# Both attention layers' work items issued in another order, fillers of TensorE included

## The reference, cut to what matters

```python
for layer in range(DEPTH):                      # DEPTH = 2
    h = h + hybrid_mixer(rms_norm(h, attn_norm[layer]), positions, layer, w_in[layer], ...)
    hn = rms_norm(h, ffn_norm[layer])
    h = h + (swiglu(hn, ...) if layer % 2 == 0 else moe_ffn(hn, ...))
return rms_norm(h, final_norm)

def hybrid_mixer(h, ...):
    (q_a, k_a, v_a, q_i, k_i, w_i, q_b, k_b, v_b, c_q, c_kv, k_r) = split(h @ w_in)
    o_a = dsa_attention(q_a, k_a, v_a, q_i, k_i, w_i)   # top 64 keys of a score, by w_i
    o_b = diff_attention(q_b, k_b, v_b, lam, ...)       # softmax minus lam * softmax, then a norm
    o_c = mla_attention(q_nope, q_rope, k_nope, k_rope, v_c)
    return concat(o_a, o_b, o_c) @ w_out
```

## Time and profile before

| | |
|---|---|
| median of 3 runs | 1509.1 us (1507.15 to 1510.11) |
| the profiled execution | 1507.44 us |
| its span, first to last instruction | 1505.7 us |
| PE busy | 1479.6 us (98%) |
| DVE busy | 1233.9 us (82%) |
| ACT busy | 1036.7 us (69%) |
| attention of layer 0 | from the start to about 149 us |
| dense part | to about 388 us |
| attention of layer 1 | to about 538 us |
| experts | from there to the end |

### The profile page before, as it was taken

One profiled execution on the slowest core, in us unless ns is written; L12 is line 12 of the kernel. 1 busy time (PEld: TensorE's weight loads), 2 busy tenths in 40 slices (PEclk: granted clock), 3 DMA queues, 4 the chain that ended last, 5 costly groups with the idle time before them and its releaser, 6 DMA issues.

```text
span 1505.7 us, 18848 instructions
## 1 busy us (share of the span) xinstructions
PE 1479.6 (98%) x7112; PEld 1233.6 (82%) x7112; DVE 1233.9 (82%) x1499; ACT 1036.7 (69%) x1355; POOL 107.9 (7%) x185
## 2 busy tenths in 40 slices
...
GB/s 286 204 57 57 244 178 213 168 196 151 126 169 92 58 239 395 374 358 400 358 370 391 366 364 396 356 362 376 382 368 388 371 372 371 384 382 369 414 389 114
DMA packets 46317, 436.86 MB, mean 290 GB/s; under 512 B 4112, under 2 KB 10640, under 8 KB 22032
## 3 DMA queue, kind: packets, MB, share of 16 engines
...
...
## 4 chain that ended last, share of the span: by engine, by line
PE 95%; DVE 3%; ACT 1%; issue 1%; DMA 0%; POOL 0%; POOLq 0%; ACTq 0%; SPq 0%; DVEq 0%
PE pair L936 51%; PE work L936 34%; PE work L908 3%; PE pair L1006 2%; PE pair L908 2%; PE work L1080 1%; PE work L923 1%; PE work L1214 1%; DVE arena L1727 0%; ACT w_hi L1306 0%; DMA ring<-in_w_in 0%; DVE w_lo L1659 0%; DVE nmax L1758 0%; DVE arena L1744 0%; ACT arena L1324 0%
## 5 line engine op out<-in xcount | busy, mean ns | idle before, releaser
L1659 DVE TENSOR_TENSOR w_lo<-ring,w_hi 128x1024 fp32r<-128x1024 f32 (+3 forms) x810 | 960.9, 1215 | 199.3 <-ACT w_hi L1306 186.1
L1306 ACT ACTIVATE w_hi<-ring 128x1024 fp32r<-128x1024 f32 (+3 forms) x810 | 838.5, 1052 | 300.8 <-PE pair L936 123.8
L936 PE MATMUL pair<-w_hi,hnT_hi 128*128 128x512 f32 x672 | 265.1, 395 | 1.7 <-DVE hnT_lo L2026 0.9
L936 PE MATMUL pair<-w_hi,hnT_lo 128*128 128x512 f32 x672 | 262.0, 390 | 0.0
L936 PE MATMUL pair<-w_lo,hnT_hi 128*128 128x512 f32 x672 | 261.5, 389 | 0.0
L936 PE MATMUL work<-w_hi,hidT_hi 128*128 128x512 f32 x552 | 215.1, 390 | 2.6 <-DVE hidT_lo L1960 1.4
L936 PE MATMUL work<-w_lo,hidT_hi 128*128 128x512 f32 x552 | 214.8, 389 | 0.0
L936 PE MATMUL work<-w_hi,hidT_lo 128*128 128x512 f32 x552 | 214.8, 389 | 0.0
L936 PE MATMUL pair<-w_hi,xU_hi 128*128 128x512 f32 x448 | 177.1, 395 | 0.0
L936 PE MATMUL pair<-w_hi,xU_lo 128*128 128x512 f32 x448 | 174.8, 390 | 0.0
L936 PE MATMUL pair<-w_lo,xU_hi 128*128 128x512 f32 x448 | 174.3, 389 | 0.0
...
## 6 DMA issues: line engine op xcount, KB each, us to landing
...
```

Source lines behind the costliest of these rows:

```text
L936: mm = pe.matmul(b, lhs[x_part][k + kk], w[w_part][:, kk, :], start=(first and kk == 0 and i == 0), stop=(last and kk == 1 and i == 2))
L1306: return act.activation(o, i, ACT.Copy)
L1659: dve.tensor_tensor(lo, raw, hi.bitcast(F32), ALU.subtract).then_inc(lo_done, 1)
```

## The change

The strings in `LISTS` are replaced by others. They hold the same items, 16 fillers per layer among them, in another order, and the fillers are numbered anew. No item is added or removed, and nothing else in the file differs, except that the text is two lines shorter, so that every line below it has a number two less. The end of layer 0's list, before and after:

```diff
-TK.1.4 CB.dsa.0.1 TP.dsa.0.1 U.diff.1.0 U.diff.1.1 O.dsa.0.0 FL.14 TP.mla.1.3 D2.0 CB.diff.1.0 U.diff.1.3
-O.dsa.0.1 FL.3 CB.diff.1.1 TP.diff.1.0 O.mla.1.3 TK.1.5 OT.0.1 OT.0.0 TK.1.6 TP.diff.1.1 O.diff.1.0 TK.1.7
-U.dsa.1.0 U.dsa.1.1 CB.diff.1.3 O.diff.1.1 WO.0.0 TP.diff.1.3 TP.dsa.1.0 O.diff.1.3 TP.dsa.1.1 D1.1 SP.25
...
+TP.diff.1.1 TK.1.5 O.diff.1.0 TP.mla.1.3 TK.1.6 O.diff.1.1 OT.0.0 OT.0.1 U.diff.1.3 TK.1.7 U.dsa.1.1 U.dsa.1.0
+CB.mla.1.3 CB.diff.1.3 WO.0.0 TP.diff.1.3 O.mla.1.3 SP.24 D1.1 CB.dsa.1.1 TP.dsa.1.1 O.diff.1.3 TP.dsa.1.0 SP.25 SP.26
```

More of the change, by code:

```diff
@@ L37 @@
 LISTS = ("""
[L38 to L47, removed]
@@ L48 @@
-CB.diff.0.0 O.diff.0.1 TK.1.0 CB.diff.1.2 O.mla.0.1 TK.0.7 TP.diff.0.0 U.dsa.0.0 U.dsa.0.1 O.diff.0.0 TK.1.1
-TP.diff.1.2 CB.dsa.0.0 U.mla.1.3 D1.0 FL.13 TK.1.2 TP.dsa.0.0 FL.8 O.diff.1.2 FL.15 AT.1 TK.1.3 CB.mla.1.3
-TK.1.4 CB.dsa.0.1 TP.dsa.0.1 U.diff.1.0 U.diff.1.1 O.dsa.0.0 FL.14 TP.mla.1.3 D2.0 CB.diff.1.0 U.diff.1.3
-O.dsa.0.1 FL.3 CB.diff.1.1 TP.diff.1.0 O.mla.1.3 TK.1.5 OT.0.1 OT.0.0 TK.1.6 TP.diff.1.1 O.diff.1.0 TK.1.7
-U.dsa.1.0 U.dsa.1.1 CB.diff.1.3 O.diff.1.1 WO.0.0 TP.diff.1.3 TP.dsa.1.0 O.diff.1.3 TP.dsa.1.1 D1.1 SP.25
@@ L53 @@
-CB.dsa.1.1 SP.26 SP.27 CB.dsa.1.0 O.dsa.1.0 D2.1 O.dsa.1.1 WO.0.1 OT.1.1 OT.1.0 NF1.0 XF.0.1 SP.28 XF.0.0
-WO.1.0 SP.29 WO.1.1 FL.10 SP.30 NF1.1 FL.9 FL.6 FL.11
-""", """
-N1.0 X.0.0 X.0.1 SP.0 SP.1 N1.1 SP.2 SP.3 SP.4 SP.5 X.1.0 PC.0 X.1.1 C1.0 SP.6 C2.0 SP.7 PC.1 CT.0 PA.1 R.kr.1
-R.kr.0 KV.0.1 QC.0.1 C1.1 QC.0.0 KV.0.0 SP.8 PA.0 C2.1 CT.1 R.c.0 MQ.0.1 MK.0.0 MK.0.1 SP.9 SP.10 SP.11 MQ.0.0
-QC.1.0 KV.1.0 SP.12 SP.13 PB.1 U.mla.0.1 QC.1.1 SP.14 U.mla.0.0 U.mla.0.3 KV.1.1 PB.0 R.c.1 MQ.1.0 MK.1.0
@@ L59 @@
[L59 to L73, removed]
+N1.0 X.0.1 X.0.0 SP.0 SP.1 N1.1 SP.2 SP.3 FL.0 X.1.0 X.1.1 SP.4 SP.5 FL.1 FL.2 PC.0 SP.6 SP.7 AN PC.1 C1.0 PA.0 C1.1
@@ new lines @@
+C2.0 R.kr.1 R.kr.0 C2.1 PA.1 CT.0 CT.1 KV.0.1 SP.8 R.c.0 SP.9 SP.10 R.c.1 KV.0.0 QC.0.0 SP.11 QC.0.1 PB.1 MQ.0.1
+MK.0.1 R.a.1 MQ.0.0 MK.0.0 SP.12 KV.1.0 QC.1.0 QC.1.1 U.mla.0.2 SP.13 KV.1.1 PB.0 MK.1.1 SP.14 TP.mla.0.2 SP.15 R.a.0
+U.mla.0.0 MQ.1.0 SP.16 CB.mla.0.0 MQ.1.1 U.mla.0.3 SP.17 SP.18 MK.1.0 CB.mla.0.3 PI.0 TP.mla.0.0 CB.mla.0.2 SP.19
+SP.20 R.i.0 SP.21 PI.1 R.b.0 PK.0 SP.22 U.mla.1.0 PK.1 O.mla.0.0 KIT.0 SP.23 IT.0 TP.mla.1.0 O.mla.0.2 U.idx.0.0
+TP.mla.0.3 U.idx.0.1 CB.mla.1.0 U.idx.0.2 R.b.1 U.idx.0.3 BT.0 U.mla.1.1 O.mla.1.0 U.mla.1.2 TK.0.0 U.diff.0.2 FL.3
```

26 lines of the change are left out of this document (added).

## The result

The changed kernel takes 1519.4 us in the median (1518.5 to 1521.3), the kernel before 1508.9 us beside it: a ratio of 1.0073, with a 95% interval of 1.0058 to 1.0088. It is slower by 10.5 us where 2.4 us less were forecast, and lies above the top of the range. The execution profiled took 1518.52 us; its page begins its first part with

The account below looks back on a forecast made before the run. PE was taken as the bound except in each attention layer's second stretch, where DVE is. Gains of 0.4 us (layer 0) and 2.0 (layer 1) sum to 2.4 us: 1506.7 us, range 1503.0 to 1512.5, counted as the same.

Parts of the forecast that it names:

- it is DVE that sets the end of this stretch: Second stretch, first index score to last maximum of `dsa`: DVE is the bound, so no gain booked if PE's dips shrink.
- PE has time over there, which the fillers use up: Second stretch of each attention layer: PE has spare time beside DVE and falls to half clock for 5.35 and 10 us.
- PE becomes the bound in the second stretch: Rival, slower: half-clock dips fall where DVE waits for logits; 1514.4 us for both layers, 1511.7 taken; chance 0.20.
- the same number of fillers: Second stretch: argument against PE becoming the bound, an unchanged filler count that leaves PE room.
- The half clock costs nothing: Second stretches: PE's two half-clock dips cost nothing much now, as DVE is busy in them; no gain booked.
- Layer 0, first stretch: Projections, where DVE waits for PE: fillers moved to PE's waits, against PC.0 starting later; 0.3 us less.
- Layer 0, second stretch: First index score to WO.0.0, on DVE: 1.06 us less work, so WO.0.0 starts 1.05 us earlier.
- a new order brings waits of its own: Layer 1, second stretch: reason for booking only half, 0.5 us, of DVE's removable waits of about 0.9 us.
- Layer 0, third stretch: From WO.0.0 on, PE is the bound: O.mla.1.3 now comes behind WO.0.0, which gives 0.9 us back.
- Layer 1, first stretch: Projections: PC.1's 0.52 us wait goes, against 0.45 us for O.mla.1.3 ahead of the first index score; sum zero.
- Layer 1, second stretch: First score to last U.dsa.1, on DVE: same work, only waits of about 0.9 us can go; 0.5 us less.
- Layer 1, third stretch: Last transposes of `dsa` start with the exponential, then the same work, 3.8 us, to WO.0.1; 1.5 us less.
- POOL: Both layers: rotations taken as hidden beside PE's projections; if a rotation were delayed, the gain shrinks from 2.4 to 1.3 us.

Follow-up runs that it names:

- e5: The changed kernel with fillers (useless transposes) added ahead of PE's waits in both second stretches, nine in layer 0 and twelve in layer 1: 1509.0 us, ratio 1.0009.
- e8: e5 without four of its added layer-1 fillers: 1507.6 us, ratio 0.9997 to the kernel before.
- e7: The kernel before without the fillers of its second stretches, 7 left out of layer 0 and 10 of layer 1: 1517.7 us, ratio 1.0067.
- e4: The kernel before with ten fillers added in PE's idle waits, four in layer 0 and six in layer 1: 1508.4 us, ratio 1.0006.
- e3: The changed kernel with four fillers added in layer 1 ahead of TP.diff.0.3, where PE stood idle: 1519.1 us, ratio 1.0072.
- e2: Layer 0's list from the change, layer 1's from the kernel before: 1514.6 us, ratio 1.0038.
- e6: The changed kernel with four of layer 1's top-k steps moved forward into DVE's waits, PE's order unchanged: 1521.6 us, ratio 1.0091.
- e1: Layer 0's list from the kernel before, layer 1's from the change: 1516.1 us, ratio 1.0060.
- e11: e8 with two pieces of layer 0 as before, the opening and O.mla.1.3 ahead of WO.0.0: 1508.3 us, ratio 1.0010.

## Why the prediction was wrong, step by step

**The step that failed is the term that was put at nothing: "it is DVE that sets the end of this stretch", so the half clock of PE costs nothing, in the new order as in the old.** DVE waited 3.4 and 8.0 us for PE, and the second stretches, forecast 1.05 and 0.5 us shorter, became 3.15 and 7.33 us longer. "PE has time over there, which the fillers use up" was read from the waits ahead of the dips; behind them PE had none left.

Of the rival "PE becomes the bound in the second stretch" the mechanism came true at both places, with its sign of recognition (DVE waits over 3 us for PE). Its size did not. It was taken from "if that dip is as long as now (5.35 and 10 us)", which gave 7.7 us and 1514.4 for both layers; the prediction took 1511.7 for the case, one layer's dip, and that is within the 3 us which it counts as the same. The dips became 13.7 and 20.5 us, and the loss 10.5. And its chance was cut to 0.20 by "the same number of fillers", a count over the stretch. Their places were what mattered, as e5 and e8 show. Between TP.diff.0.3 and TP.diff.1.0 in layer 1 the list of before has nine fillers and the new one two; in layer 0 six and four. That could be read from the lists beforehand. The chances don't quite follow either: 2.4 us less with a spread of 1.2 leaves more than a fifth beyond 3 us, 0.31 if the spread is a standard deviation. It changes nothing in the outcome.

Runs show this from both sides: added fillers alone take the new order from a ratio of 1.0073 to 0.9997 (e8), and taken-out fillers alone bring the old order to 1.0067 (e7).

**"The half clock costs nothing" was right for the dips it had before it (e4), and wrong as a rule.** Against the same stretch at full clock (e4 or e8), in the executions profiled:

| list and layer | half clock, us | second stretch longer by, us |
|---|---|---|
| before, layers 0 and 1 | 6.8 and 10.3 | 0.0 and 0.0 |
| after, layer 0 | 13.7 | 3.4 |
| e3, layer 0 | 13.6 | 3.9 |
| e3, layer 1 | 13.7 | 5.4 |
| e2, layer 0 | 17.1 | 5.0 |
| e6, layer 0 | 20.5 | 7.1 |
| e1, layer 1 | 20.5 | 6.5 |
| after, layer 1 | 20.5 | 7.3 |
| e7, layer 0 | 23.9 | 6.1 |
| e7, layer 1 | 27.3 | 3.8 |
| e6, layer 1 | 27.3 | 10.0 |

Four rows are of one and the same list, layer 0 of the change: 13.7, 13.6, 17.1 and 20.5 us cost 3.4, 3.9, 5.0 and 7.1, so about half a us for each us more. That the first part of a dip is free as long as DVE has a backlog fits this and the four lines of e7, but no run moved the backlog by itself. e3's 13.7 us in layer 1 cost more than the 13.7 of layer 0 and fell where DVE was busy for little more than half of the time. e7's layer 1 is cheap: its first 9 us were DVE's, and PE had ten fillers less to do there, 4.5 us by the 0.45 us of one, an estimate. e6's 10.0 us hold the cost of its moved top-k steps too, and I can't part them.

**Layer 0, first stretch** (0.3 us less): measured 0.17 less. **Layer 0, second stretch** (1.05 less): at full clock 0.2 less (e5, e8). DVE has 1.06 us less to do, but its waits rose: in e5, from 77 to 124 us,

```profile
DVE nmax L1758 <- PE pair L1009: 0.6, 2, 0.4
...
DVE arena L1727 <- ACT arena L1442: 0.6, 2, 0.4
DVE arena L1725 <- ACT arena L1442: 0.5, 1, 0.5
DVE nmax L1758 <- PE pair L1006: 0.4, 1, 0.4
```

come to 2.1 us, where the same view of before has 1.4 (the two of the earlier trace rows and two of 0.2; the prediction says 1.2). This is the part "a new order brings waits of its own", which I had applied to layer 1 alone. **Layer 0, third stretch** (0.9 back): 0.6 back, and e11 shows that moving O.mla.1.3 away from there doesn't return it. **Layer 1, first stretch** (zero): 0.02. **Layer 1, second stretch** (0.5 less): at full clock 0.0 (e8). **Layer 1, third stretch** (1.5 less): 0.75 less. In the changed kernel:

```profile
513.71 0.63 PE L906 MATMUL work<-ident,arena 128*128 128x128 f32 x4
...
515.03 0.63 PE L906 MATMUL work<-ident,arena 128*128 128x128 f32 x4
...
519.12 0.47 PE L934 MATMUL work<-w_hi,hnT_hi 128*128 128x512 f32 x1
```

From the end of WO.0.0 to the last transposes of `dsa` it is now 1.32 us (513.71 to 515.03), against 2.37 before (502.77 to 505.14): 1.05 less, about what the eight transposes that were taken out need. No PE wait is listed there before or after, so the exponential held nothing up, and there was no more to gain. And from those transposes to WO.0.1 it is 4.09 us instead of 3.81, not "the same work, 3.8 us", which gives 0.28 back; what takes it is open. **POOL**: no wait for a rotation is among those that made the loss, and no run tested whether POOL and DVE hold each other up. With the clock held (e8's column) the change gives 0.5 us up to the experts, against 2.4 forecast, and neither can be told from nothing.

**What the clock does.** PE was busy for 20.00 of 20.00 us from 481 to 501 us and the granted clock stayed at 0.50. The Trainium skill, page "TensorE: Matmul & The Clock Gate", section "What's actually happening", says that activity releases the throttle. Here the trace agrees that idle PE comes ahead of the fall (1.89 us ahead of TP.diff.0.3), and not that a PE which the profile shows as busy gets its clock back by that: the measurement decides. It rose again at 501.5 us, within a run of twelve transposes of 128x128 that began at 500.80; whether they brought it back no run tests.
